# Fetching each expert pair's token rows by indirect DMA, and splitting every gate chunk, in a one-core hybrid attention, mLSTM and mixture-of-experts layer

## The chip, the cores and the metric

The kernel runs on one core of one Trainium2 chip, in one launch. The metric is the device time of that launch in microseconds; the kernel before has a median of 1496.52 us over three runs (1495.86 to 1496.99). All stage times below are counted in us from the start of the profiled span.

## The reference, cut to what matters

256 tokens of width 2048 go through one layer in float32: a big input projection, sparse attention, an mLSTM, a gated mix and an output projection, a layer norm (h), and then the part that the change touches:

```python
def hier_moe(x, w_grp, b_grp, w_exp, b_exp, w_gate, w_up, w_down):
    grp_prob = softmax(x @ w_grp + b_grp)              # 4 groups, the best one is taken
    g_p, g_idx = top_k(grp_prob, 1)
    e_p, e_idx = top_k(softmax(in_grp), 2)             # 2 of the 4 experts of that group
    e_p = e_p / sum(e_p)
    h = silu(x @ w_gate[e]) * (x @ w_up[e]) * combine[e]   # e = 0..15, FF = 512
    return h @ w_down[e], summed over the experts

ff = hier_moe(h, ...)
ple = (p @ w_ple) * sigmoid(h @ w_ple_gate)            # w_ple_gate is 2048 x 2048
h = layer_norm(DN_ALPHA * h + ff + ple, ln2_g, ln2_b)
```

Each token takes 2 of 16 experts, so 512 token slots are in use out of 16 x 64 that the kernel keeps. On the inputs used, the experts receive 13, 21, 18, 18, 34, 39, 35, 48, 30, 34, 32, 24, 40, 51, 38 and 37 tokens.

## The kernel before, in words

**Projections.** Until about 916 us the weights of the projections pass through a ring in SBUF; ScalarE copies each tile to a rounded high part (float32r), VectorE subtracts it for the low part, and TensorE makes three float32r matmuls (high x high, low x high, high x low) in place of one float32 matmul. The change leaves that part alone.

**Between the projections and the experts** (916 to 947 us) the rows are normalized (`RES`, which SyncE also writes to the output tensor in DRAM as a parking place, line 452), turned on TensorE (`row_turn`, line 875) and kept as `hT`; the router is computed; VectorE makes `selg`, a 0/1 matrix of tokens against the 64 slots of each of a group's 4 experts (`select`, line 2247). The rows are also split into `h1h` (ScalarE, `high`, line 1502) and `h1l` (VectorE, `h1_low`, line 2155).

**The experts** are taken in 8 pairs, two pairs to a group. `up(n)` has 8 slots: each slot loads 1 MiB of one weight of each of the two experts (2 MiB) and multiplies it with `xg`, the turned rows of the pair's slots; `down(n)` has 4 slots of 2 MiB. The written order is up 0, up 1, down 0, up 2, down 1, up 3, ... down 5, up 7, down 6, down 7. `xg` is made by selection products: for a group, `gather_pair` (line 976) multiplies `h1h` and `h1l` with `selg`, 8 pairs of feature tiles of 8 float32r matmuls with 256 columns, and ScalarE and VectorE add gain and bias while they copy the result out (`gained`, lines 1563 and 2262). Group 0 is gathered before and inside up 0 (`first_pairs`), group g at the start of down(2g-2), between its slots. `scatter` (lines 1107, 1108) adds a pair's outputs to the token rows with the turned matrix `selT`.

**The gate product** h @ w_ple_gate is cut into 16 chunks: one loaded early (`EW`), 15 that travel in the ring at fixed slots (`CHUNKS_IN`). Chunks 0 to 8 are float32 matmuls with `hT` (`ple_rows`, line 928), which the trace records as two instructions each; chunks 9 to 14 are split like the projections (`gate_high` line 1592, `gate_low` line 2339, `split_rows` lines 950 to 952), after `turned_high` and `turned_low` have split `hT` itself in down 4.

**The ring.** `moe_ring` has 8 places of 1 MiB and 207 loads pass through it, in the order in which TensorE uses them. SyncE issues load m once TensorE has used load m-8:

```python
            def ring_load(m, dst, src):
                ...
                else:
                    sp.wait_ge(ring_used, m - RING + 1)
                sp.dma_start(dst, src).then_inc(ring_in[m % RING], 16)
```

So the first 8 loads are in before the experts start, and the other 199 follow TensorE's progress. No planner decides anything: each engine's order is the order of the code.

**The end** (1456 to 1498 us): the last four down slots with scatters between them (`down_last`, line 1092), `last_scatter`, the statistics, the second norm and the output.

Of the kernel before, what the change touches and what calls it, by code (L numbers as in the profile page):

```python
# [68 lines left out]
SPLIT_FROM = 9  # L69
# [68 lines left out]
def build(nc, x, p, w_in, kv_norm, w_ukv, m_i_bias, m_f_bias, w_proj_a, w_proj_m, w_out, ln1_g, ln1_b,  # L138
          w_grp, b_grp, w_exp, b_exp, w_gate, w_up, w_down, w_ple, w_ple_gate, ln2_g, ln2_b, out):
    with ExitStack() as ctx:  # L140
# [46 lines left out]
        GH = at("gate_hi", [2, D], Z1 + 16384, F32R)  # L187
# [34 lines left out]
        xg = at("xg", [KT, EPG * CAP], Z3)  # L222
# [43 lines left out]
        lgc, lbc, fold = tiny(KT), tiny(KT), tiny(32)  # L266
        flag = at("flag", [2], ZS + 3072, I32)

# [10 lines left out]
        ident_ready, const_ready, identr_ready = sem("ident_ready"), sem("const_ready"), sem("identr_ready")  # L279
# [27 lines left out]
        h1_hi, h1_lo, res_gain, res_ready = sem("h1_hi"), sem("h1_lo"), sem("res_gain"), sem("res_ready")  # L307
# [190 lines left out]
        def _(pl):  # L498
# [50 lines left out]
            def deviation(n):  # L549
# [6 lines left out]
            deviation(1)  # L556
            g.iota(iota[:], pattern=[[1, CAP]], base=0, channel_multiplier=0,
                   allow_small_or_imprecise_dtypes=True).then_inc(iota_ready, 1)
# [6 lines left out]
        def _(pe):  # L565
# [366 lines left out]
            def ple_chunk(at, b):  # L932

                i = CHUNK_OF[at]
                pe.wait_ge(ple_ev, i + 1)
                if i < SPLIT_FROM:
                    ple_rows(landed_load(("ple", i, 0, 0)), b, (i + EARLY) % 4, True, True).then_inc(ring_used, 1)
                else:
                    split_rows(i, b).then_inc(ring_used, 1)

            def split_rows(i, b):

                j, s = i - SPLIT_FROM, LOAD_AT["ple", i, 0, 0] % RING
                pe.wait_ge(split_hi, j + 2)
                pe.wait_ge(split_lo, j + 2)
                for t in range(4):
                    k, c = 4 * ((i + EARLY) % 4) + t, slice(t * NC, t * NC + NC)
                    for a in range(NT):
                        r = slice(a * P, a * P + P)
                        mm(B[b + a][:, :], hTh[:, k, r], GH[:, j % 2, c], start=t == 0, stop=False)  # L950
                        mm(B[b + a][:, :], hTl[:, k, r], GH[:, j % 2, c], start=False, stop=False)
                        last = mm(B[b + a][:, :], hTh[:, k, r], RL0[:, s, c], start=False, stop=t == 3)
# [10 lines left out]
            def weight_table(bank, s):  # L963

                for pair in range(2):
                    for a in range(NT):
                        last = mm(B[bank][:, 4 * pair:4 * pair + 4], selg[:, a, pair * P:pair * P + P].bitcast(F32),
                                  combw[:, 4 * a:4 * a + 4], start=a == 0, stop=a == 1)
                last.then_inc(s, 1)

# [15 lines left out]
            def gather(g, pairs):  # L986

                for i in pairs:
                    if i < 2:
                        pe.wait_ge(selT_c, 2 * g + i + 1)  # L990
                    elif i % 2:
                        pe.wait_ge(g_dve, 4 * (g - 1) + i // 2)
                    else:
                        pe.wait_ge(g_act, 8 + 4 * (g - 1) + i // 2)
                    gather_pair(i, B[i % 2]).then_inc(g_mm, 1)

            def first_pairs(q):
# [9 lines left out]
            def up_slot(w, i, b0, e0):  # L1007

                for t in range(4):
                    k = 4 * (i // 2) + t  # L1010
                    for e in range(2):
                        last = mm(B[b0 + i % 2][CAP * e:CAP * e + CAP, :], xg[:, k, (e0 + e) * CAP:(e0 + e) * CAP + CAP],  # L1012
# [3 lines left out]
            def up(n):  # L1016

                b, other = 2 * (n % 2), 2 * ((n + 1) % 2)
                if n and n % 2 == 0:
                    pe.wait_ge(g_act, 8 + 4 * (n // 2))  # L1020
                    pe.wait_ge(g_dve, 4 * (n // 2))
                if n:
                    pe.wait_ge(ple_ev, max(chunks_in("up", n - 1) + chunks_in("down", n - 2), default=-1) + 2)
                for i in range(UP_SLOTS):
                    w = landed_pair("up", n, i)
                    if n == 0 and i % 2 == 0:
                        pe.wait_ge(g_act, i + 2)
                    up_slot(w, i, b, 2 * (n % 2)).then_inc(ring_used, 2)
                    if n == 0 and i in (1, 3):
                        if i == 1:  # L1030
                            pe.wait_ge(combined, 1)
                            weight_table(5, selT_mm)
                        first_pairs(i // 2 + 2)
                    if n == 0 and i == 6:
                        ple_rows(EW[:, 0, :], 2, 0, True, True, (1, 2, 3)).then_inc(early_used, 1)
                    if i == 2:
                        if n:
# [30 lines left out]
            def down(n):  # L1068

                pe.wait_ge(e_Tc, n + 1)  # L1070
                if n:
                    pe.wait_ge(y_add, 2 * CHUNKS * n)
                for k in range(DOWN_SLOTS):
# [4 lines left out]
                    if n % 2 == 0 and n < NP - 2:  # L1078
                        if k == 0:
                            pe.wait_ge(ple_ev, max(chunks_in("up", n + 1)) + 2)  # L1080
                            group_rows(n // 2 + 1)
# [86 lines left out]
            with pe.Else():  # L1168
                pe.wait_ge(split_lo, len(CHUNKS_IN) - SPLIT_FROM + 2)
                pe.wait_ge(y_add, 2 * CHUNKS * NP)  # L1170
                for r in range(3):
                    with pe.Fori(0, GROUPS) as g:
# [10 lines left out]
                        for pair in range(2):  # L1183
# [8 lines left out]
                            for i in range(UP_SLOTS):  # L1192
                                up_slot(landed_over(i), i, 0, 2 * pair).then_inc(ring_used, 2)
# [18 lines left out]
        def _(ac):  # L1212
# [286 lines left out]
            def high(a):  # L1499

                ac.wait_ge(z_ready, NT)
                fn(h1h[:, a, :, :].rearrange("p t q -> p q t"), RES[:, a, :].rearrange("p (q t) -> p q t", t=KT),
                   ACT.Copy).then_inc(h1_hi, 1)
# [10 lines left out]
            high(0)  # L1514
            pp_copy(4)
            pp_copy(5)
            high(1)
            pp_copy(6)
            pp_copy(7)
# [25 lines left out]
            def weight_table(ready, r0, bank, s, weights):  # L1545

                ac.wait_ge(ready, r0 + 2)
                for e in range(2):
                    last = fn(weights[CAP * e:CAP * e + CAP, :], B[bank][CAP * e:CAP * e + CAP, e:e + 12:6], ACT.Copy)
                last.then_inc(s, 1)  # L1550

            def group_tables(g):
# [4 lines left out]
                row_table(selT_mm, 2 * g, 0, selT_c, g % 2)  # L1557
                weight_table(selT_mm, 2 * g, 1, selT_c, cg[:, 2 * (g % 2):2 * (g % 2) + 2])

            def gained(i, b):  # L1560

                for k in (2 * i, 2 * i + 1):
                    last = fn(xg[:, k, :], b[:, k % 2 * TOK:k % 2 * TOK + TOK], ACT.Identity, bias=lbc[:, k:k + 1],
# [3 lines left out]
            def gathered(g):  # L1567

                used("up", 2 * g - 1, UP_SLOTS - 1)
                for i in range(0, 8, 2):  # L1570
                    ac.wait_ge(g_mm, 8 * g + i + 1)
                    gained(i, B[0]).then_inc(g_act, 1)

# [937 lines left out]
```

## Time and profile before

| | before |
|---|---|
| median of 3 runs | 1496.52 us |
| the profiled execution, its own time | 1499.46 us |
| its span, first to last instruction | 1497.7 us |
| TensorE busy | 1464.7 us (98%) |
| VectorE, ScalarE, GpSimd busy | 706.8, 513.2, 57.1 us |
| bytes moved by DMA | 405.92 MB, mean 271 GB/s |
| mean granted TensorE clock | 0.998 |

TensorE's busy time is an average over a projection part, in which the DMA engines are about half busy, and the expert part, in which the page's DMA digits stand at 9 throughout. A matmul's printed duration is longer than the time from one to the next, because they are pipelined: pitches are read from start times.

### The profile page before, as it was taken

To read this page: it belongs to the slowest core of one execution; us is meant where nothing else is said; L and a number is where in the kernel's file an instruction comes from. 1 tells how busy PE (TensorE), PEld (TensorE's weight loads), DVE (VectorE), ACT (ScalarE), POOL (GpSimd) and SP (SyncE) were. 2 spreads that over 40 slices of the span, in tenths; PEclk is the share of its full clock that TensorE was granted. 3 is DMA by queue.
4 is the path that set the end of the run, shared out by engine and by line. 5 is a ranking of instruction groups with operands and counts; after the bars stand their busy time and mean duration, and the time that the engine had idled before them with its cause. 6 is when DMAs were issued, how large, how long until landed. Compare 5 with 4: busy or idle time off the path is not lost.

```text
span 1497.7 us, 16743 instructions
## 1 busy us (share of the span) xinstructions
PE 1464.7 (98%) x6572; PEld 997.8 (67%) x6572; DVE 706.8 (47%) x974; ACT 513.2 (34%) x690; POOL 57.1 (4%) x63
## 2 busy tenths in 40 slices
PE   9999999999999999999999999999989998999998
PEld 7887788888788888888888886534424533444443
DVE  5546676467656665454555655421221221143336
ACT  4444444455554454434445343401000201031111
POOL 0000000043300000000000000000000000000000
PEclk9999999999999999999999999999999999999999
DMA  9654586754454675565566957599999999999994
GB/s 310 200 172 165 168 238 198 218 194 157 145 171 141 202 237 190 187 197 195 196 204 231 368 202 257 241 414 421 407 399 411 389 390 418 410 389 418 416 401 173
DMA packets 138287, 405.92 MB, mean 271 GB/s; under 512 B 14296, under 2 KB 18016, under 8 KB 113248
## 3 DMA queue, kind: packets, MB, share of 16 engines
q1 hardware_dynamic: 129472, 396.52, 72.6%
q10 hardware_dynamic: 8736, 8.33, 1.7%
q8 instruction: 51, 0.84, 0.2%
q14 instruction: 28, 0.23, 0.1%
HBM read 392.76 MB, written 4.20 MB: 265 GB/s over the span
## 4 chain that ended last, share of the span: by engine, by line
PE 90%; DMA 7%; DVE 1%; ACT 1%; issue 1%; SPq 0%; POOL 0%; DVEq 0%; POOLq 0%; ACTq 0%
PE bank L574 19%; PE bank L575 19%; PE bank L579 19%; PE bank L1012 11%; PE bank L1064 5%; PE bank L928 4%; DMA moe_ring<-in_w_gate_dram 4%; DMA moe_ring<-in_w_ple_gate_dram 2%; PE bank L976 2%; PE bank L1092 1%; PE bank L1107 1%; PE bank L1108 1%; DMA moe_ring<-in_w_down_dram 1%; PE bank L733 1%; PE bank L950 1%; PE bank L755 1%
## 5 line engine op out<-in xcount | busy, mean ns | idle before, releaser
L1715 DVE TENSOR_TENSOR w_lo<-w_ring,w_hi 128x1024 fp32r<-128x1024 f32 (+1 forms) x312 | 381.5, 1225 | 286.0 <-ACT w_hi L1228 284.9
L1228 ACT ACTIVATE w_hi<-w_ring 128x1024 fp32r<-128x1024 f32 (+1 forms) x312 | 327.3, 1051 | 328.9 <-PE bank L579 328.9
L574 PE MATMUL bank<-w_hi,xT_hi 128*128 128x512 f32 (+1 forms) x864 | 344.3, 399 | 1.8 <-ACT w_hi L1228 1.8
L575 PE MATMUL bank<-w_hi,xT_lo 128*128 128x512 f32 (+1 forms) x864 | 334.6, 387 | 0.0
L1012 PE MATMUL bank<-moe_ring,xg 128*64 128x512 f32 x1024 | 226.4, 595 | 9.8 <-DMA moe_ring<-in_w_gate_dram 7.1
L579 PE MATMUL bank<-w_lo,xT_hi 128*128 128x512 f32 (+1 forms) x864 | 229.2, 387 | 0.0
L574 PEld LDWEIGHTS bank<-w_hi,xT_hi 128*128 128x128 f32 x864 | 162.3, 188 | 38.6 <-issue 4.6
L575 PEld LDWEIGHTS bank<-w_hi,xT_lo 128*128 128x128 f32 x864 | 162.4, 188 | 32.8 <-issue 1.9
L579 PEld LDWEIGHTS bank<-w_lo,xT_hi 128*128 128x128 f32 x864 | 161.5, 188 | 33.2 <-DVE w_lo L1715 0.4
L1012 PEld LDWEIGHTS bank<-moe_ring,xg 128*64 128x64 f32 x1024 | 72.9, 137 | 156.3 <-issue 155.9
L1064 PE MATMUL bank<-moe_ring,moe_hiddenT 128*64 128x512 f32 x448 | 100.5, 595 | 3.8 <-DMA moe_ring<-in_w_down_dram 3.7
L2318 DVE TENSOR_TENSOR res<-res,bank 128x512 f32<-128x512 f32 x62 | 38.5, 681 | 104.4 <-issue 80.3
L1064 PEld LDWEIGHTS bank<-moe_ring,moe_hiddenT 128*64 128x64 f32 x448 | 31.7, 137 | 63.7 <-issue 62.4
L928 PE MATMUL bank<-moe_ring,h1T 128*128 128x512 f32 x144 | 63.4, 593 | 0.0
L2281 DVE TENSOR_TENSOR ple_sig<-bank,ple_sig 128x512 f32<-128x512 f32 x24 | 15.5, 686 | 81.3 <-PE bank L928 58.3
L574 PE MATMUL bank<-w_hi,mixT_hi 128*128 128x512 f32 x128 | 50.1, 391 | 0.0
L575 PE MATMUL bank<-w_hi,mixT_lo 128*128 128x512 f32 x128 | 49.8, 389 | 0.0
L574 PE MATMUL bank<-w_hi,yaT_hi 128*128 128x512 f32 x128 | 49.8, 389 | 0.0
L575 PE MATMUL bank<-w_hi,yaT_lo 128*128 128x512 f32 x128 | 49.8, 389 | 0.0
L574 PE MATMUL bank<-w_hi,ymT_hi 128*128 128x512 f32 x128 | 49.8, 389 | 0.0
L575 PE MATMUL bank<-w_hi,ymT_lo 128*128 128x512 f32 x128 | 49.8, 389 | 0.0
L928 PEld LDWEIGHTS bank<-moe_ring,h1T 128*128 128x128 f32 x144 | 27.2, 190 | 31.6 <-issue 31.0
(292 smaller groups left out, 1360.9 us busy)
## 6 DMA issues: line engine op xcount, KB each, us to landing
w_ring<-in_w_in_dram SPq DMA_DIRECT2D x103, 1024.0 KB, 5.0
moe_ring<-in_w_gate_dram SPq DMA_DIRECT2D x64, 1024.0 KB, 9.8
moe_ring<-in_w_up_dram SPq DMA_DIRECT2D x64, 1024.0 KB, 10.6
moe_ring<-in_w_down_dram SPq DMA_DIRECT2D x64, 1024.0 KB, 10.5
w_ring<-in_w_proj_a_dram SPq DMA_DIRECT2D x16, 1024.0 KB, 5.0
w_ring<-in_w_proj_m_dram SPq DMA_DIRECT2D x16, 1024.0 KB, 5.0
w_ring<-in_w_out_dram SPq DMA_DIRECT2D x16, 1024.0 KB, 5.3
moe_ring<-in_w_ple_gate_dram SPq DMA_DIRECT2D x15, 1024.0 KB, 13.1
```

What stands on the lines that cost most here:

```text
L574: mm(b, lh(k, m), WH[:, s, kk, 0:width], start=start and kk == 0, stop=False)
L575: mm(b, ll(k, m), WH[:, s, kk, 0:width], start=False, stop=False)
L579: last = mm(b, lh(k, m), WL[:, s, kk, 0:width], start=False, stop=stop and kk == 1)
L733: last = mm(B[4 + j][:, r * w:r * w + w], aqT[:, 4 * (u % 4) + 2 * j + r, a * P:a * P + P], kT[:, 0:w], start=True, stop=True)
L928: ins = mm(B[b + a][:, :], hT[:, k, a * P:a * P + P], w[:, t * NC:t * NC + NC], start=first and t == 0, stop=last and t == 3)
L976: last = mm(b[:, kk * TOK:kk * TOK + TOK], src[:, a, 2 * i + kk, :], selg[:, a, :], start=part == 0 and a == 0, stop=part == 1 and a == 1)
L1012: last = mm(B[b0 + i % 2][CAP * e:CAP * e + CAP, :], xg[:, k, (e0 + e) * CAP:(e0 + e) * CAP + CAP], w[e][:, t * NC:t * NC + NC], start=k = ...
L1064: last = mm(B[4 + c][CAP * e:CAP * e + CAP, :], src[:, k, CAP * e:CAP * e + CAP], w[e][:, c * NC:c * NC + NC], start=k == 0, stop=k == 3)
L1228: fn(WH[:, h % 4, :, 0:width], W32[:, h // 2, 2 * (h % 2):2 * (h % 2) + 2, 0:width], ACT.Copy).then_inc(hi_ready, 1)
L1715: v.tensor_tensor(WL[:, h % 4, :, 0:width], W32[:, h // 2, 2 * (h % 2):2 * (h % 2) + 2, 0:width], WH[:, h % 4, :, 0:width].bitcast(F32), A ...
L2281: last = v.tensor_tensor(psg[:, a, :], B[b + a][:, :], psg[:, a, :], ALU.add)
L2318: v.tensor_tensor(r, r, B[b0 + a][:, :], ALU.add).then_inc(y_add, 1)
```

## The change

The selection products go. Instead, a list of token numbers per slot is made, and GpSimd fetches each pair's 128 slot rows (8 KiB each) from the output tensor in DRAM by an indirect DMA, which leaves out the slots whose list entry is 4096 or more. For groups 1 to 3 an empty slot gets 4096; for group 0 the list is a plain product, so an empty slot gets 0 and row 0 is fetched for it: 128 rows for each of pairs 0 and 1. TensorE turns the fetched rows, 16 transposes of 128x128 to a pair, and ScalarE and VectorE copy them into `xg` with gain and bias. All 15 ring chunks of the gate product are split in three passes; `hT` is split before up 0 and `gate_hi` has one buffer for two.

```diff
-SPLIT_FROM = 9
+FAR = 4096
...
-        GH = at("gate_hi", [2, D], Z1 + 16384, F32R)
+        ZG = at("z_slots", [D], Z1 + 16384)
+        GH = at("gate_hi", [D], Z1 + 24576, F32R)
...
+            for n in range(NP):
+                pl.wait_ge(listed, n // 2 + 1)
+                if n == 0:
+                    pl.wait_ge(z_moved, 16)
+                    pl.wait_ge(pp_mm, 8)
+                elif n == 1:
+                    pl.wait_ge(split_hi, 1)
+                    pl.wait_ge(split_lo, 1)
+                    pl.wait_ge(early_used, 1)
+                    pl.wait_ge(rows_in, 16)
+                else:
+                    pl.wait_ge(g_mm, 4 * n)
+                g.indirect_dma_start((ZG if n else ZG0)[:], None, out[0], bass.IndirectOffsetOnAxis(ap=idx[:, n:n + 1], axis=0),
+                                     bounds_check=TOK - 1, oob_is_err=False).then_inc(rows_in, 16)
...
-                if i < SPLIT_FROM:
-                    ple_rows(landed_load(("ple", i, 0, 0)), b, (i + EARLY) % 4, True, True).then_inc(ring_used, 1)
-                else:
-                    split_rows(i, b).then_inc(ring_used, 1)
+                split_rows(i, b).then_inc(ring_used, 1)
...
+            def pair_turn(n, q, b0):
 
                 if q == 0:
-                    pe.wait_ge(pp_c, 8)
-                pe.wait_ge(h1_lo, q + 1)
-                for i in (2 * q, 2 * q + 1):
-                    if i >= 2:
-                        pe.wait_ge(g_act, i - 1)
-                    gather_pair(i, B[6 + i % 2]).then_inc(g_mm, 1)
+                    pe.wait_ge(rows_in, 16 * (n + 1))
+                if q >= 2:
+                    pair_evacuated(n, q - 2)
+                elif n == 1:
+                    pair_evacuated(0, q + 2)
+                z = (ZG if n else ZG0).rearrange("p (q t) -> p t q", t=KT)
+                for kk in range(4):
+                    last = nc.tensor.transpose(B[b0 + q % 2][:, kk * P:kk * P + P], z[:, 4 * q + kk, :], ident[:])
+                last.then_inc(g_mm, 1)
...
             def down(n):
...
-                        if k < 3:
-                            gather(n // 2 + 1, ((0, 1), (2, 3, 4), (5, 6, 7))[k])
...
+                    if k >= 2 and n < NP - 2:
+                        pe.wait_ge(e_hid, n + 2)
+                        for q in (2 * k - 4, 2 * k - 3):
+                            pair_turn(n + 2, q, 2 * ((n + 1) % 2))
...
             pe.wait_ge(sel_ready, 1)
+            first_list()
             row_table(4, selT_mm)
-            pe.wait_ge(h1_hi, NT)
-            first_pairs(0)
-            first_pairs(1)
+            ple_rows(EW[:, 0, :], 2, 0, True, True, (1, 2, 3)).then_inc(early_used, 1)
+            pe.wait_ge(pp_c, 8)
+            for q in range(4):
+                pair_turn(0, q, 6)
...
             select(0)
-            for q in range(4):
-                h1_low(q)
+            slot_list(0)
             combine()
             overflow()
+            turned_low()
+            gained(0, 1, 7)
+            gained(0, 3, 7)
             residual(0)
             residual(1)
+            gained(1, 1, 7)
+            gained(1, 3, 7)
```

Where the instructions stand. TensorE between the router and up 0, before: the selection products (L976) stand ahead of the first weights (L1012).

```order
L928 MATMUL bank<-ple_early,h1T 128x512
L960 MATMUL bank<-ident_r,moe_sel 128x128 [waits sel_ready]
L960 MATMUL bank<-ident_r,moe_sel 128x128 x3
L976 MATMUL bank<-moe_sel,h_hi 128x256 [waits h1_lo,pp_copied,h1_hi]
L976 MATMUL bank<-moe_sel,h_hi 128x256
L976 MATMUL bank<-moe_sel,h_lo 128x256 x2
...
L1012 MATMUL bank<-moe_ring,xg 64x512 [waits gathered_act,ring_in1,ring_in0]
L1012 MATMUL bank<-moe_ring,xg 64x512 x7
```

The same place after the change (L1001 is the slot list, L952 the rest of the early chunk, L1034 a turn of fetched rows, L1042 the first weights):

```order
L1001 MATMUL bank<-small,moe_sel 128x1 [waits sel_ready]
L1001 MATMUL bank<-small,moe_sel 128x1 x3
L986 MATMUL bank<-ident_r,moe_sel 128x128 x4
L952 MATMUL bank<-ple_early,h1T 128x512 x6
L1034 MATMUL bank<-ident,z_slots_first 128x128 [waits slot_rows_in,pp_copied]
L1034 MATMUL bank<-ident,z_slots_first 128x128 x7
L1034 MATMUL bank<-ident,z_slots_first 128x128 [waits gathered_act]
L1034 MATMUL bank<-ident,z_slots_first 128x128 x3
L1034 MATMUL bank<-ident,z_slots_first 128x128 [waits gathered_dve]
L1034 MATMUL bank<-ident,z_slots_first 128x128 x3
L1042 MATMUL bank<-moe_ring,xg 64x512 [waits gathered_act,ring_in1,ring_in0]
```

The rest of the early chunk moved from slot 6 of up 0 to a place ahead of it, and the first weights now stand behind the landing of pair 0's rows and behind two evacuations.

TensorE in down 0, after the change: the tables of group 1 stand ahead of the first slot, and the turns of pair 2 behind slots 2 and 3 (L1092 is a down slot).

```order
L986 MATMUL bank<-ident_r,moe_sel 128x128 [waits sel_ready,ple_evac,e_T_copied]
L986 MATMUL bank<-ident_r,moe_sel 128x128 x3
L993 MATMUL bank<-small,moe_sel 128x5 x4
L1092 MATMUL bank<-moe_ring,moe_hiddenT 64x512 [waits ring_in2,ring_in1]
...
L1092 MATMUL bank<-moe_ring,moe_hiddenT 64x512 [waits ring_in6,ring_in5]
L1092 MATMUL bank<-moe_ring,moe_hiddenT 64x512 x7
L1034 MATMUL bank<-ident,z_slots 128x128 [waits slot_rows_in,e_hid]
L1034 MATMUL bank<-ident,z_slots 128x128 x7
L1092 MATMUL bank<-moe_ring,moe_hiddenT 64x512 [waits ring_in0,ring_in7]
L1092 MATMUL bank<-moe_ring,moe_hiddenT 64x512 x7
```

Before, 64 selection matmuls stood between the slots at this place, and the tables behind slot 0.

## Rows read from the trace of the kernel before

**Rows 1.** The page, part 2: share of the span in 40 slices.

```profile
PE   9999999999999999999999999999989998999998
DMA  9654586754454675565566957599999999999994
```

**Rows 2.** The stages: busy time of each engine, granted clock, DMA share, GB/s.

```profile
core 0: us, PE busy (x) PEld busy (x) DVE busy (x) ACT busy (x) POOL busy (x), PEclk, DMA share, GB/s
940.00:951.00 11.00, 10.29 (x60) 6.34 (x60) 9.67 (x20) 6.32 (x13) 0.00 (x0) 1.00 0.01 2
952.00:1466.00 514.00, 494.04 (x2190) 217.52 (x2187) 130.24 (x198) 73.69 (x120) 0.00 (x0) 1.00 1.00 406
1096.00:1126.00 30.00, 24.74 (x114) 8.97 (x111) 3.03 (x8) 2.67 (x5) 0.00 (x0) 1.00 1.02 418
1240.00:1265.00 25.00, 19.90 (x88) 7.97 (x85) 4.96 (x8) 2.66 (x5) 0.00 (x0) 1.00 1.02 418
1366.00:1420.00 54.00, 50.19 (x226) 23.63 (x223) 14.31 (x18) 9.65 (x13) 0.00 (x0) 1.00 1.02 418
1085.00:1096.00 11.00, 11.00 (x48) 3.81 (x48) 5.97 (x12) 1.65 (x2) 0.00 (x0) 1.00 0.94 358
```

**Rows 3.** DMA from 952 to 1466 us: packets and bytes.

```profile
DMA packets 37454, 208.92 MB, mean 406 GB/s; under 512 B 3178, under 2 KB 3178, under 8 KB 14900
```

**Rows 4.** TensorE's waits from 951 to 1473 us: total, times, longest.

```profile
PE bank L1012 <- DMA moe_ring<-in_w_gate_dram: 7.1, 6, 1.3
PE bank L950 <- DVE gate_lo L2339: 5.5, 4, 2.5
PE bank L1064 <- DMA moe_ring<-in_w_down_dram: 3.7, 3, 1.3
PE bank L1012 <- DMA moe_ring<-in_w_up_dram: 2.6, 2, 1.3
```

**Rows 5.** Timeline of TensorE: start us, us, engine, line, what, count [idle before].

```profile
923.33 3.98 PE L875 MATMUL bank<-ident,res 128*128 128x128 f32 x32 [0.29 <-DVE res L2144]
...
940.80 0.96 PE L960 MATMUL bank<-ident_r,moe_sel 128*128 128x128 f32 x4
...
946.70 7.09 PE L1012 MATMUL bank<-moe_ring,xg 128*64 128x512 f32 x32
953.71 1.06 PE L967 MATMUL bank<-small,moe_sel 128*128 128x4 f32 x8
...
976.28 5.42 PE L928 MATMUL bank<-ple_early,h1T 128*128 128x512 f32 x12
...
1034.51 0.40 PE L976 MATMUL bank<-moe_sel,h_lo 128*128 128x256 f32 x2
1034.74 0.40 PE L976 MATMUL bank<-moe_sel,h_hi 128*128 128x256 f32 x2
...
1126.99 7.03 PE L928 MATMUL bank<-moe_ring,h1T 128*128 128x512 f32 x16
...
1351.88 0.39 PE L950 MATMUL bank<-gate_hi,h1T_hi 128*128 128x512 f32 x1
...
1357.41 7.09 PE L1012 MATMUL bank<-moe_ring,xg 128*64 128x512 f32 x32
...
1472.74 3.65 PE L1092 MATMUL bank<-moe_ring,moe_hiddenT 128*64 128x512 f32 x16
```

**Rows 6.** SyncE's DMA issues in order of time.

```profile
923.30 0.40 SPq L452 DMA_DIRECT2D out_dram<-res  x1
950.39 0.81 SPq L445 DMA_DIRECT2D moe_ring<-in_w_gate_dram  x2
```

**Rows 7.** The page, part 6: DMA issues, KB each, median us from issue to landing.

```profile
moe_ring<-in_w_down_dram SPq DMA_DIRECT2D x64, 1024.0 KB, 10.5
w_ring<-in_w_proj_a_dram SPq DMA_DIRECT2D x16, 1024.0 KB, 5.0
```

**Rows 8.** VectorE's timeline from the router to 950 us.

```profile
938.75 1.39 DVE L2247 TENSOR_SCALAR moe_sel<-iota,small 128x64 fp32r<-128x64 f32 x8
940.06 7.96 DVE L2155 TENSOR_TENSOR h_lo<-res,h_hi 128x512 fp32r<-128x512 f32 x8
947.92 0.17 DVE L2219 TENSOR_REDUCE small<-small 128x2 f32<-128x8 f32 x1
```

**Rows 9.** Groups of ScalarE and VectorE instructions: busy us, mean ns of one.

```profile
L1667 ACT ACTIVATE rstd_diagonal<-ident,small 128x128 f32<-128x128 f32 x2 | 0.8, 402 | 7.3 <-POOL small L561 7.3
L2331 DVE TENSOR_TENSOR h1T_lo<-h1T,h1T_hi 128x1024 fp32r<-128x1024 f32 x4 | 4.6, 1220 | 2.9 <-ACT h1T_hi L1579 2.9
L1592 ACT ACTIVATE gate_hi<-moe_ring 128x1024 fp32r<-128x1024 f32 x12 | 12.0, 1048 | 54.9 <-DMA moe_ring<-in_w_ple_gate_dram 54.9
```

More of the change, by code:

```diff
@@ L949, in split_rows @@
                         r = slice(a * P, a * P + P)
-                        mm(B[b + a][:, :], hTh[:, k, r], GH[:, j % 2, c], start=t == 0, stop=False)
-                        mm(B[b + a][:, :], hTl[:, k, r], GH[:, j % 2, c], start=False, stop=False)
+                        mm(B[b + a][:, :], hTh[:, k, r], GH[:, c], start=t == 0, stop=False)
+                        mm(B[b + a][:, :], hTl[:, k, r], GH[:, c], start=False, stop=False)
+                pe.wait_ge(split_lo, i + 2)
+                for t in range(4):
+                    k, c = 4 * ((i + EARLY) % 4) + t, slice(t * NC, t * NC + NC)
+                    for a in range(NT):
+                        r = slice(a * P, a * P + P)
                         last = mm(B[b + a][:, :], hTh[:, k, r], RL0[:, s, c], start=False, stop=t == 3)
@@ L966, in weight_table, with first_list @@
                     for a in range(NT):
-                        last = mm(B[bank][:, 4 * pair:4 * pair + 4], selg[:, a, pair * P:pair * P + P].bitcast(F32),
-                                  combw[:, 4 * a:4 * a + 4], start=a == 0, stop=a == 1)
+                        last = mm(B[bank][:, 5 * pair:5 * pair + 5], selg[:, a, pair * P:pair * P + P].bitcast(F32),
+                                  wtk[:, 5 * a:5 * a + 5], start=a == 0, stop=a == 1)
                 last.then_inc(s, 1)
+            def first_list():
+                for pair in range(2):
+                    for a in range(NT):
+                        last = mm(B[5][:, 480 + pair:481 + pair], selg[:, a, pair * P:pair * P + P].bitcast(F32), tok[:, a:a + 1],
+                                  start=a == 0, stop=a == 1)
+                last.then_inc(list_mm, 1)
             def gather_pair(i, b):
@@ L1513, in _ @@
                 last.then_inc(hT_act, 1)
[L1514 to L1519, printed above, removed]
+            for q in range(4):
+                pp_copy(4 + q)
+                last = turned_high(q)
+            last.then_inc(split_hi, 1)
             def used(kind, n, i):
@@ L1548, in weight_table @@
                 for e in range(2):
-                    last = fn(weights[CAP * e:CAP * e + CAP, :], B[bank][CAP * e:CAP * e + CAP, e:e + 12:6], ACT.Copy)
+                    last = fn(weights[CAP * e:CAP * e + CAP, :], B[bank][CAP * e:CAP * e + CAP, e:e + 14:7], ACT.Copy)
                 last.then_inc(s, 1)
@@ L1557, in group_tables, with gained @@
                 row_table(selT_mm, 2 * g, 0, selT_c, g % 2)
+                ac.wait_ge(listed, g + 1)
                 weight_table(selT_mm, 2 * g, 1, selT_c, cg[:, 2 * (g % 2):2 * (g % 2) + 2])
-            def gained(i, b):
+            def gained(n, q, b):
+                ac.wait_ge(g_mm, 4 * n + q + 1)
+                for kk in range(4):
+                    k = 4 * q + kk
+                    last = fn(xg[:, n % 2, k, :], B[b][:, kk * P:kk * P + P], ACT.Identity, bias=lbc[:, k:k + 1],
+                              scale=lgc[:, k:k + 1])
+                last.then_inc(g_act, 1)
@@ L1562, in gained, with gained_over @@
+            def gained_over(i, b):
                 for k in (2 * i, 2 * i + 1):
-                    last = fn(xg[:, k, :], b[:, k % 2 * TOK:k % 2 * TOK + TOK], ACT.Identity, bias=lbc[:, k:k + 1],
+                    last = fn(xgo[:, k, :], b[:, k % 2 * TOK:k % 2 * TOK + TOK], ACT.Identity, bias=lbc[:, k:k + 1],
                               scale=lgc[:, k:k + 1])
                 return last
[L1567 to L1572, printed above, removed]
@@ L2361, in _ @@
             for kind, n in ORDER[:-1]:
+                if kind == "down" and n % 2 == 0 and n < NP - 2:
+                    slot_list(n // 2 + 1)
                 for slot in range(SLOTS_OF[kind]):
@@ L2372, in _ @@
                         ple_part((i + EARLY) // 4)
-                    if kind == "up" and n >= 6 and slot == 2:
-                        gate_low(10 if n == 6 else 13)
                 if kind == "up":
                     hidden(n)
-                    if n >= 6:
-                        gate_low(11 if n == 6 else 14)
                     if n % 2 == 0 and n < NP - 2:
```

178 lines of the change are left out of this document (81 added, 97 removed).

## The prediction

> **What bounds the kernel now.** I began with the page's slices: TensorE shows 9 nearly everywhere, but from slice 27 on the DMA digits are 9 as well [rows 1]. So the expert part is short of two things at once, and the view that tells them apart is the stages. Where TensorE waits for weights (1096 to 1126, 1240 to 1265, 1366 to 1420 us), the DMA engines move 418 GB/s at a share of 1.02, and no stage shows more: that is their ceiling here. Over the whole of 952 to 1466 us they move 406 GB/s at 1.00, TensorE being busy for 494 of the 514 us; where TensorE holds the ring places (1085 to 1096) it is 358 at 0.94 [rows 2]. The waits agree: TensorE waits 13.4 us in all for weights, never over 1.3 us at once, and 5.5 us for VectorE's low part of a gate chunk [rows 4]. The bytes of the stage, 208.92 MB [rows 3], are just the 199 loads of 1 MiB (208.7 MB) that follow TensorE, so the last of them lands at about 1466 us, and TensorE begins the last down slot only at 1472.74 [rows 5]. The two engines are thus near a tie: a stream that could end earlier by its rate, and TensorE a little behind it at the end.
>
> **What TensorE saves.** A selection matmul follows the last by 0.12 us (1034.51 to 1034.74 for two, [rows 5]); 256 of them are 30.7 us. In their place come 8 x 16 transposes at 3.98/32 = 0.124 us [rows 5], 15.9 us. A float32 chunk is 16 records in 6.96 us (7.03 of which the last end overlaps), a split one 1351.88 to 1357.41 less a restart, 5.45 us [rows 5]: 9 chunks give 13.6 us. The slot list adds 1 us, being as large as the weight table of 1.06 us [rows 5]. Together TensorE has 27 us less to do.
>
> **What that is worth is read from the stream,** not from that sum. Four terms.
>
> *The start, +5.0 us.* The first ring issue of the stage comes at 950.39 [rows 6], when slot 0 of up 0, begun at 946.70 [rows 5], is used. After the change slot 0 waits for this: `selg` ready at 940.1 [rows 8]; the list product 1 us, to 941.8; its copy, to 942.1; the fetch of 1 MiB. No row shows an indirect DMA. A load takes 5.0 us from issue to landing in the projections and 10.5 in a full queue [rows 7], and the engines stand idle here (2 GB/s, [rows 2]), so it lands between 944.6 (its bytes alone at 418 GB/s) and 952.6; I take 947.1, the nearest row. TensorE fills that time with 5.42 us of the early chunk [rows 5], to 947.6, which is work moved and no loss. Then two turns, to 948.6. What is late next is VectorE: after the list copy come the combine and overflow steps (2 us), the low part of `hT`, 4 x 1.22 = 4.9 us [rows 9], to 950, then four evacuations of 128x128, under 0.4 each by ScalarE's 128x128 copy of 402 ns [rows 9], to 951.3, then the last turn: up 0 begins at 951.7, not 946.7. The selection products inside up 0 and the early chunk there are gone, but the stream doesn't gain from it: it starts with the first used slot. Pair 1's fetch is issued at about 950 and lands before the ring asks for much, so it costs nothing; without that gap it would be 2.5 us.
>
> *The stream's idle time, -15.0 us.* 208.7 MB take 499 us at 418 GB/s, against 514 now. With 27 us less work TensorE releases places fast enough nearly everywhere.
>
> *The rows, +11.0 us.* GpSimd fetches pairs 2 to 7 while the stream runs. The 16 experts' counts put 442 token rows of 8 KiB into them, 3.62 MB: 8.7 us at 418 GB/s. That is the lower end. The upper is that each of the six costs as much as a whole load of 1 MiB, 6 x 2.5 = 15.0 us: taken slots are always the first of each expert's 64, so the same partitions get the rows each time, and a load of 128 partitions has landed only when its slowest share has. I take 11, between them.
> The Trainium skill has a price for that: its page "DMA: Bandwidth & Descriptors", section "The descriptor swizzle", gives each DMA engine eight fixed partitions, by which the busiest one (partitions 64 to 67 and 96 to 99) gets 42 of the 442 rows where the mean is 27.6. By that skill page the term would be an estimated 13 us and the sum 2 us longer; no row here shows an engine by itself.
>
> *The end, -5.0 us.* TensorE is now 6.6 us behind the last landing. With the saved work it should be 1 to 2 us behind: the last four down slots and three scatters between them take it as long as 8 loads take, and chunk 14 ahead of them still has its wait, up to 2.5 us [rows 4], since ScalarE makes that chunk's high part (2 x 1.05 us, [rows 9]) only after the hidden turn.
>
> *A rest, +1.0 us,* for chunks behind which the ring still stands full. Of the other edits, the turns of pair n+2 behind slots 2 and 3 of down n wait for fetched rows and ScalarE's evacuations; an even pair's fetch is issued at the start of that down, some 10 us (three slots of 3.5 us) ahead, against 5.0 to 10.5 us for landing [rows 7], and a short wait there is covered by the stream, which has eight places in hand. If that cover is gone each of three such waits costs what it lasts. ScalarE's and VectorE's nine more chunk splits (2.1 and 2.4 us each, [rows 9]) fall beside TensorE's slots; both are under 26% busy there [rows 2]. GpSimd has nothing else in its queue until the last norm.
>
> Sum: 5.0 - 15.0 + 11.0 - 5.0 + 1.0 = **-3.0 us**. The profiled execution took 1499.46 us, so the same sum gives 1496.5 there; that execution lies 2.9 us above the median of 1496.52, from which the forecast is **1493.5 us**. A measurement of this kernel can tell about 0.2% (3 us) from no change, so this forecast lies on that bound.
>
> **Rivals.**
> 1. *The gather is late (slower).* From the landing, up 0 needs two turns (1.0), an evacuation by each of ScalarE and VectorE (1.6) and two more turns (1.0), 3.6 us; so from a landing at 948 us on, 6 us after the list, the rows and not VectorE set the start, and every us of theirs moves the whole stream by one. GpSimd has never issued such a DMA in this trace, and it has to make 128 row addresses. At 10 us from list to landing (952.1) up 0 begins at 955.7, 4 us more, 1497.5; at 13 us it is 7 more, 1500.5. For it: an operation without a row. Against: idle DMA engines. Chance of over 9 us, 0.22, with some 1500.5.
> The Trainium skill's page "SBUF — State Buffer", section "SBUF: two separate sides", warns that GpSimd can't write descriptors while VectorE holds the port that the two share. VectorE's instructions beside the first fetch are tiny ones until 945 us, then four of 1.22 us [rows 9] until 950. As a mechanism of this kernel: a fetch whose addresses are written only behind these lands at about 952.5 (950 and the 2.5 us of its bytes), and up 0 begins 4.4 us later than I have it, 1498. No row here shows GpSimd held up by VectorE, and I give that 0.05 of the 0.22.
> 2. *The rows cost as whole loads,* by the partitions or because empty slots aren't left out after all: the rows' term is 15 or more, 1497.5, no change. For it: the same slots are full each time. Against: eight loads in flight even things out. 0.20.
> 3. *TensorE's saving comes through whole:* 27 us less 5, 1474. The waits for weights of 13.4 us [rows 4] and the 1.02 share speak against it. 0.03.
> 4. *The stream fills up better than I think,* rows at their 8.7 us and the start only 3 us later: -8 us, 1488.5. 0.13.
>
> The forecast's own case has 0.42 and its range is 1490.5 to 1496.5. The range for 8 in 10 reaches to half of rival 4 and into rival 1: 1487 to 1502. Faster by over 0.2%: half of the forecast's case and a bit (0.25), rivals 3 and 4 (0.16), 0.41. Within 0.2%: the rest of the forecast's case (0.17), most of rival 2 (0.16) and a little of rival 1 (0.02), 0.35. Slower: 0.24.
>
> **What would show it.** After the change TensorE should be clearly less busy from 952 us on, with some 35 to 50 us of waits for weights in pieces under 2 us, and the DMA engines at 415 to 420 GB/s over the whole stage. Up 0 should begin at 951 to 953 us, the wait ahead of it ending with VectorE's evacuation or with the rows. The bytes of the stage should be near 212.5 MB; near 215 would say that empty slots are fetched. The last down slot should begin within 2 us of the last landing. The prediction is wrong if GB/s stays at 406, if up 0 begins after 956, or if TensorE waits for fetched rows by more than 3 us in a down.

## The result, and the profile after

The changed kernel is slower: 1505.3 us (median of 4 runs, 1504.21 to 1507.19) against 1496.19 us (4 runs, 1491.39 to 1496.99), a ratio of 1.0075 with a 95% interval of 1.0063 to 1.0088. The forecast was 1493.5 us with a range up to 1502; the time lies above it. The profiled execution took 1505.65 us, its span is 1503.9 us (before: 1497.7).

The page of the changed kernel, parts 1 to 3:

```profile
PE 1451.9 (97%) x6524; PEld 1000.3 (67%) x6524; DVE 730.1 (49%) x1028; ACT 526.9 (35%) x730; POOL 65.6 (4%) x73
...
DMA  8654586754444776565566956699999999999994
...
DMA packets 139440, 411.65 MB, mean 274 GB/s; under 512 B 14750, under 2 KB 18470, under 8 KB 113702
...
q0 software_dynamic: 1152, 5.72, 1.0%
```

Queue q0 is new: 5.72 MB are 698 rows of 8 KiB, the 256 of group 0 and the 442 of the others. Empty slots are left out, as the change says.

The stages of the changed kernel (same columns as in [rows 2]):

```profile
940.00:953.60 13.60, 10.58 (x44) 6.24 (x42) 8.20 (x22) 5.54 (x12) 2.27 (x2) 0.96 0.32 99
953.60:958.50 4.90, 4.90 (x19) 1.61 (x20) 1.79 (x5) 4.45 (x5) 0.00 (x0) 0.76 0.38 154
960.00:1472.00 512.00, 475.63 (x2138) 218.11 (x2135) 151.82 (x247) 87.89 (x156) 5.95 (x6) 0.98 1.02 415
```

The stream is full now: 415 GB/s at 1.02 where [rows 2] had 406 at 1.00, and TensorE is busy for 476 of 512 us instead of 494 of 514. That part of the forecast is there, though TensorE was to save 27 us and not 18; part of what is missing is its granted clock, 0.98 over this stage and 1.00 before (see the last section). The start is not as forecast. TensorE around up 0 (start us, us, engine, line, what, count, idle before):

```profile
942.57 5.37 PE L952 MATMUL bank<-ple_early,h1T 128*128 128x512 f32 x12
949.81 1.14 PE L1034 MATMUL bank<-ident,z_slots_first 128*128 128x128 f32 x8 [1.87 <-DMA z_slots_first<-out_dram,slot_rows]
952.09 1.67 PE L1034 MATMUL bank<-ident,z_slots_first 128*128 128x128 f32 x8 [1.15 <-ACT xg L1595]
953.69 8.20 PE L1042 MATMUL bank<-moe_ring,xg 128*64 128x512 f32 x32
...
1478.66 3.65 PE L1121 MATMUL bank<-moe_ring,moe_hiddenT 128*64 128x512 f32 x16
```

and the engines ahead of it, VectorE's list, GpSimd's fetch and SyncE's first issue of the stage:

```profile
942.27 0.16 DVE L2272 CAST slot_rows<-bank 128x2 int32<-128x2 f32 x1 [2.04 <-PE bank L1001]
...
943.38 1.28 POOL L580 DMA_INDIRECT z_slots_first<-out_dram,slot_rows  x1 [22.36 <-DVE slot_rows L2272]
...
958.50 0.81 SPq L451 DMA_DIRECT2D moe_ring<-in_w_gate_dram  x2
```

The rows are there at 949.8 us, 7.4 us after the list, of which 1 us passes before GpSimd begins. Up 0 begins at 953.69, not at 946.70, and its first two slots take 8.1 us instead of 7.0: the granted clock is 0.76 in that stretch, partly at 1.2 GHz and partly at 2.4. The first ring issue comes 8.1 us later than in [rows 6]. The last down slot begins 5.9 us later than in [rows 5].

Where TensorE waits in the changed kernel, from 940 us on:

```profile
PE bank L1042 <- issue: 12.8, 7, 3.3
PE bank L971 <- ACT gate_hi L1616: 8.8, 8, 2.7
PE bank L1042 <- DMA moe_ring<-in_w_up_dram: 8.6, 8, 2.4
PE bank L1092 <- DMA moe_ring<-in_w_down_dram: 4.8, 4, 2.6
```

"Issue" means that the profile names no releaser; these waits stand at up slots, as those for weights do, and I count them as such. The wait for `gate_hi` is one for ScalarE's high part of a gate chunk.

### The profile page after: what moved, and what is told of

Read it like the earlier page. It is cut to its first block, busy times and chain, and to the rows that moved or that the text cites. A ratio compares the mean times of both kernels' runs of the same rounds, so it can differ in the third digit from the quotient of the medians.

```text
span 1503.9 us, 16809 instructions
## 1 busy us (share of the span) xinstructions
PE 1451.9 (97%) x6524; PEld 1000.3 (67%) x6524; DVE 730.1 (49%) x1028; ACT 526.9 (35%) x730; POOL 65.6 (4%) x73
## 3 DMA queue, kind: packets, MB, share of 16 engines
q0 software_dynamic: 1152, 5.72, 1.0%
## 4 chain that ended last, share of the span: by engine, by line
PE 88%; DMA 8%; issue 1%; ACT 1%; DVE 1%; SPq 0%; POOL 0%; POOLq 0%; ACTq 0%; DVEq 0%
PE bank L598 19%; PE bank L599 19%; PE bank L603 19%; PE bank L1042 13%; DMA moe_ring<-in_w_up_dram 6%; PE bank L1092 4%; PE bank L971 2%; PE bank L978 2%; PE bank L972 2%; ACT gate_hi L1616 1%; PE bank L1121 1%; DMA moe_ring<-in_w_ple_gate_dram 1%; DMA moe_ring<-in_w_down_dram 1%; PE bank L757 1%; PE bank L1136 1%
## 5 line engine op out<-in xcount | busy, mean ns | idle before, releaser
L1042 PE MATMUL bank<-moe_ring,xg 128*64 128x512 f32 x1024 | 237.6, 615 | 22.5 <-issue 12.8
L1042 PEld LDWEIGHTS bank<-moe_ring,xg 128*64 128x64 f32 x1024 | 76.5, 141 | 166.9 <-issue 166.1
L1092 PE MATMUL bank<-moe_ring,moe_hiddenT 128*64 128x512 f32 x448 | 101.4, 603 | 4.8 <-DMA moe_ring<-in_w_down_dram 4.8
L1092 PEld LDWEIGHTS bank<-moe_ring,moe_hiddenT 128*64 128x64 f32 x448 | 32.3, 138 | 65.1 <-issue 64.5
L2279 DVE TENSOR_SCALAR xg<-bank,small 128x128 f32<-128x128 f32 x64 | 21.9, 403 | 109.5 <-PE bank L1034 109.5
L1595 ACT ACTIVATE xg<-bank,small 128x128 f32<-128x128 f32 x64 | 24.1, 458 | 113.4 <-PE bank L1034 113.4
L971 PE MATMUL bank<-gate_hi,h1T_hi 128*128 128x512 f32 x120 | 48.5, 404 | 8.8 <-ACT gate_hi L1616 8.8
L1616 ACT ACTIVATE gate_hi<-moe_ring 128x1024 fp32r<-128x1024 f32 x30 | 30.0, 1048 | 76.6 <-DMA moe_ring<-in_w_ple_gate_dram 63.7
L2356 DVE TENSOR_TENSOR gate_lo<-moe_ring,gate_hi 128x1024 fp32r<-128x1024 f32 x30 | 35.3, 1218 | 35.6 <-ACT gate_hi L1616 35.6
```

The costliest lines, as they stand in the source:

```text
L971: mm(B[b + a][:, :], hTh[:, k, r], GH[:, c], start=t == 0, stop=False)
L1042: last = mm(B[b0 + i % 2][CAP * e:CAP * e + CAP, :], rows[:, k, CAP * e:CAP * e + CAP], w[e][:, t * NC:t * NC + NC], start=k == 0, stop=k ...
L1092: last = mm(B[4 + c][CAP * e:CAP * e + CAP, :], src[:, k, CAP * e:CAP * e + CAP], w[e][:, c * NC:c * NC + NC], start=k == 0, stop=k == 3)
L1616: last = fn(GH[:, c], RW[:, m % RING, c], ACT.Copy)
L2356: last = v.tensor_tensor(RL0[:, s, c], RW[:, s, c], GH[:, c].bitcast(F32), ALU.subtract)
```

## A second profile of the kernel before

The profiles differ by 6.2 us, the medians by 9.1. So I took the kernel before once more.

> The kernel before once more, for a second profile. The span of the first one is 1497.7 us where the runs of this kernel have a median of 1494 to 1496.5. If the first profile was a long execution, this one's span is 1490 to 1496 us, and the place of the difference shows what the extra us of the changed kernel's median over its profiled difference are; if the span is 1497 to 1498 again, the profiler itself adds them.

Its span is 1494.4 us. TensorE's last down slot and the second ring issue of the stage (in the first profile at 1472.74 and 953.82):

```profile
952.97 0.81 SPq L445 DMA_DIRECT2D moe_ring<-in_w_up_dram  x2
...
1469.24 3.65 PE L1092 MATMUL bank<-moe_ring,moe_hiddenT 128*64 128x512 f32 x16
```

The first profile was a long execution: 0.9 us came before the stream, 2.6 us of the rest within it. Against the second one the changed kernel's last down slot is 9.4 us later and its span 9.5 us longer, close to the difference of the medians. Below I use both.

## The experiments

Each ratio below is to runs of the kernel before that were taken beside that experiment; their medians lie between 1494.0 and 1495.3 us. Differences to the changed kernel are to its 1505.3 us, so they carry 1 to 2 us of doubt.

Three theories went in. **A:** the weight stream, from its first issue on, sets the pace as far as up 7, and TensorE's own work sets the rest (79 us from the last wait for weights to the last down slot); start, rows and end each count in full. **C:** a later start or added bytes are caught up on the way. **E:** it is TensorE's sum that counts.

**The rows of groups 1 to 3, taken away.**

```diff
-                    v.tensor_scalar(idx[:, 2 * g:2 * g + 2], B[1][:, 4:14:5], float(FAR), None, ALU.add).then_inc(listed, 1)
+                    v.tensor_scalar(idx[:, 2 * g:2 * g + 2], B[1][:, 4:14:5], 3.0 * FAR, None, ALU.add).then_inc(listed, 1)
```

> The changed kernel, except that the slot lists of groups 1 to 3 are out of range, so that pairs 2 to 7 fetch no row (3.62 MB less) and compute on stale rows. Theory A (the weight stream sets the pace up to up 7, and TensorE's own work of some 79 us sets the rest): the rows cost what their bytes take at 418 GB/s, 8.7 us, so 1497 us, with up 7 beginning 8 to 9 us sooner. Theory B (a fetch costs as much as a whole load of 1 MiB): 15 us less, 1490. Theory C (the rows ride in idle DMA time): under 3 us less, over 1502.

1495.72 us, 9.6 us less than the changed kernel. The stream begins at the same time and the last down slot 10.2 us sooner:

```profile
958.69 0.81 SPq L451 DMA_DIRECT2D moe_ring<-in_w_gate_dram  x2
...
1468.44 3.65 PE L1121 MATMUL bank<-moe_ring,moe_hiddenT 128*64 128x512 f32 x16
```

A holds, C falls for bytes. 3.62 MB cost 9.6 to 10.2 us, between their 8.7 us at 418 GB/s and 15. The six fetches are still made here, they only carry no row (from 960 to 1478 us):

```profile
q0 software_dynamic: 864, 0.00, 0.1%
z_slots<-out_dram,slot_rows POOLq DMA_INDIRECT x6, 7.4
```

So what this run takes away is the price of the rows' bytes, not that of a fetch as such. The kernel has every saving of the change and no row behind the start, and still is only level with the kernel before (1.0012, 1.0002 to 1.0022): the late start alone eats what TensorE saves.

**Empty slots fetched too.** The list column of `wtk` starts at 0 instead of -4096 and nothing is added, so empty slots name row 0.

> The changed kernel with empty slots of groups 1 to 3 listed as row 0, so that all 8 fetches move 128 rows: 326 rows or 2.67 MB more behind the start of up 0. Same output. Theory A (bytes at the stream's rate, 10 us for the 3.62 MB that are fetched now): 6.4 to 7.4 us slower than the changed kernel, 1511 to 1513. Theory B (each fetch costs as a whole load already, by its fullest partitions): under 2 us slower, 1507.

1508.7 us (1506.27 to 1510.76), 3.4 us more; in the profiles the last down slot is 5.2 us later, although the stream began 0.8 us sooner. The page says that the bytes moved:

```profile
q0 software_dynamic: 1152, 8.39, 1.4%
```

2.67 MB more cost 3.4 us by the medians and 6.0 us by the profiles (5.2 and the 0.8 us of the start). A had 6.4 to 7.4, B under 2, and the runs lie between them; the spread of four runs to a side (1506.27 to 1510.76 here) is as large as what would tell them apart. From no row to all rows the two steps together cost 13.0 us by the medians and 16.4 us by the profiles, and the 6.29 MB of both are 15.0 us at 418 GB/s. That a fetch costs anything beyond its bytes, or that the fullest partitions count, is not shown; nor is whether row 0, read 326 times, costs what other rows do.

**The wait for pair 0's rows, taken away.** `pair_turn(0, ...)` reads `RES[:, 0, :]` and leaves out `wait_ge(rows_in, ...)`; the fetch is still made.

> The changed kernel, except that pair 0's turns read rows that are in SBUF already (tokens 0 to 127) and don't wait for the fetch, which is still made; pair 0 computes on the wrong rows. Theory A: the first pair's fetch holds the start of the stream; up 0 begins at about 951.6 us instead of 953.7, held by VectorE's evacuation now, and the whole stream moves by the same 2 us; with the slow clock of the first slot gone, up to 1 us more: 1502 to 1503.5. Theory C (a later start is caught up, since the ring is full and TensorE was waiting for weights anyway): 1505, no change. If the start moves by x and the end by less than half of x, the start was not the cause.

1501.36 us, 3.9 less.

```profile
951.92 7.09 PE L1042 MATMUL bank<-moe_ring,xg 128*64 128x512 f32 x32
...
1474.66 3.65 PE L1121 MATMUL bank<-moe_ring,moe_hiddenT 128*64 128x512 f32 x16
```

Up 0 begins at 951.9, as forecast for a fetch that is in time (951.7), at full clock: its first two slots take 7.0 us. The first issue is 2.9 us sooner (955.61) and the last down slot 4.0. So 2.9 us of the 8.1 are the landing and the slow clock behind it, and the other 5 are the new chain itself. Most of the earlier start is in the landing of the last ring load too, 2.5 us sooner (1471.67 for 1474.21); the rest of the 4.0 is TensorE standing 3.0 us behind that landing in place of 4.5, for which I have no cause.

**ScalarE's order at the chunks.**

```diff
                     if n == NP - 2:
+                        gate_high(chunks_in(kind, n)[0])
                         hidden_turned(n + 1)
```

and likewise for the chunk behind slot 2 of each up.

> The changed kernel with ScalarE's order changed: the high part of a chunk behind slot 2 of an up, and of chunk 14 in down 6, is made ahead of the copy of the turned hidden rows, not behind it. Same output. Theory A (TensorE is the bound from slot 2 of up 7 on): its waits for the high part there, 0.82 us at chunk 12 and 2.67 us at chunk 14, go, so the end comes 3 us sooner, about 1502; the waits of this kind ahead of up 7 are worth nothing, the stream covers them. Theory D (the last landing sets the end): no change, 1505. Theory E (TensorE's sum of waits counts everywhere): all 8.8 us, 1496.5.

1502.36 us, 2.9 less. The wait for high parts goes from 8.8 to 2.4 us and the end gains 3 of the 6.4, those in the end part. The profile shows what is late next, the last loads:

```profile
PE bank L971 <- ACT gate_hi L1616: 2.4, 3, 1.2
...
PE bank L1121 <- DMA moe_ring<-in_w_down_dram: 0.6, 1, 0.6
```

**The fetched rows without the split chunks.** `ple_chunk` calls `ple_rows` for all 15; `h1T` isn't split, and `z_slots` lies where its high part was.

> The changed kernel with all 15 ring chunks as float32 products of h1T (6.96 us each on TensorE instead of 5.45 and no high or low parts), the fetched rows kept. Same output. Theory A: twelve of the 15 chunks lie where the stream sets the pace and cost next to nothing; the last three add 4.5 us to TensorE's end part and take its waits of 3.5 us for high parts away, so 1505 to 1508. Theory E (TensorE's sum counts): 15 x 1.5 = 22.6 us less the 8.8 us of waits, 1519.

1508.13 us, 2.8 more than the changed kernel. The split of the chunks, some 14 us of TensorE's work and 22 if it is counted over all 15, is worth 2.8 us at most: the profile's first ring issue is itself 1.0 us later (959.53), with a longer stretch of slow clock in slot 0. E falls, since it asked for 1519.

**Two of the last three chunks, done ahead of up 7.**

```diff
-CHUNKS_IN = (("up", 1, 4), ("up", 2, 2), ("up", 2, 5), ("up", 3, 2), ("up", 3, 5), ("up", 4, 2), ("up", 4, 5),
+CHUNKS_IN = (("up", 1, 4), ("up", 2, 2), ("up", 2, 5), ("down", 1, 1), ("up", 3, 2), ("up", 3, 5), ("up", 4, 2),
...
-             ("up", 5, 2), ("up", 5, 5), ("up", 6, 2), ("up", 6, 5), ("down", 5, 1), ("up", 7, 2), ("up", 7, 5),
-             ("down", 6, 1))
+             ("up", 4, 5), ("down", 3, 1), ("up", 5, 2), ("up", 5, 5), ("up", 6, 2), ("up", 6, 5), ("down", 5, 1),
+             ("up", 7, 2))
```

> The changed kernel with two of the last three gate chunks' places moved ahead: places (up 7, slot 5) and (down 6, slot 1) are given up for (down 1, slot 1) and (down 3, slot 1). Same output. Theory A (from up 7 on TensorE is the bound, ahead of it the stream is): TensorE gives up two chunks and the 2.7 us wait of chunk 14 in the end part and does them where it waits for weights; it can gain no more than its lag behind the last landing, 6.5 us, less 1: 5 us faster than the changed kernel, 1500, with the last down slot beginning within 1.5 us of the last landing. Theory E (it is TensorE's whole sum that counts): no change, 1505.

1503.29 us (1502.4 to 1505.37), 2 us less where I had 5. TensorE now does wait for the last loads:

```profile
PE bank L1092 <- DMA moe_ring<-in_w_down_dram: 3.4, 3, 1.4
PE bank L1121 <- DMA moe_ring<-in_w_down_dram: 1.7, 1, 1.7
```

so the place of the bound is as A says. But the last ring load landed 1.5 us later than in the changed kernel (1475.73 for 1474.21), of which 0.7 us is a later first issue (959.18), and part of the gain was given back. There was also less to gain than I thought: in the changed kernel the last down slot begins 4.5 us after that landing and not 6.5, and here 0.8.

**Group 0 by selection products again,** pairs 2 to 7 fetched; `h1T` is split behind up 0's products:

```diff
-            for n in range(NP):
+            for n in range(2, NP):
...
-            first_list()
             row_table(4, selT_mm)
-            ple_rows(EW[:, 0, :], 2, 0, True, True, (1, 2, 3)).then_inc(early_used, 1)
-            pe.wait_ge(pp_c, 8)
-            for q in range(4):
-                pair_turn(0, q, 6)
+            pe.wait_ge(h1_hi, NT)
+            first_pairs(0)
+            first_pairs(1)
```

> The changed kernel with group 0's rows made by selection products as before (no fetch for pairs 0 and 1), h1T split behind up 0's products, all else as changed. Same output. Theory A: the first issue of the ring goes back from 958.5 to 950.4 us and the whole stream with it, 8 us faster than the changed kernel, 1497.5, less up to 1 us for TensorE's 7 us of products. Theory C (a later start is caught up): under 3 us faster.

1498.79 us, 6.5 less than the changed kernel and 1.0033 (1.0023 to 1.0044) of the one before. The stream is back where it was and the end 4.8 us sooner:

```profile
953.62 0.81 SPq L452 DMA_DIRECT2D moe_ring<-in_w_up_dram  x2
...
1473.89 3.65 PE L1122 MATMUL bank<-moe_ring,moe_hiddenT 128*64 128x512 f32 x16
```

From the first issue to the last down slot it takes 523.7 us (from 950.2), the changed kernel 520.2: the earlier start is not passed on in full, 4.8 of 8.3 us in the profile and 6.5 by the medians (the profiled execution, 1500.78 us, is 2 us longer than this kernel's median). That TensorE's products in up 0 make the difference is likely, but wasn't tried.

**All three together.**

> Group 0 by products, the two chunk places moved ahead, and ScalarE's high parts behind slot 2 ahead of the turned hidden rows, all together. Same output. Theory A adds the two gains, 8 and 5 us, as they lie in different parts: 1492, some 3 us faster than the kernel before. Theory C and E: 1500 or more.

1494.98 us, 10.3 less than the changed kernel and level with the one before (1.0007, 0.9998 to 1.0017). I had 1492, from gains of 8 and 5 us that came out at 6.5 and 2 to 3. What was gained adds nearly in full, but it only makes good the cost.

**The same move of chunks in the kernel before.** Chunks 0 to 10 stay float32.

> The kernel before with the same two chunk places moved ahead (chunks 0 to 10 float32, 11 to 14 split, as their places ask). Same output. Theory A: there TensorE holds the ring in many stretches ahead of up 7 too, so 11 to 14 us of added work there push the stream back by most of that, and the gain at the end is used up: between 1493 and 1499. Theory F (the gain is in the tail alone and has nothing to do with the fetched rows): 5 us faster than the kernel before, 1490.

1492.59 us, 0.9987 of the kernel before (0.9976 to 0.9998), 1.4 us less than its median of 1493.99: the fastest kernel of this study, by little. I had it at 1493 to 1499, so here my theory was too gloomy: the stream of the kernel before took the added work without ending later. Its last load landed at 1465.18, as in the second profile of the kernel before (1465.20), though the stream began 1.2 us later (950.78). TensorE waits for the last loads at the end here too:

```profile
PE bank L1064 <- DMA moe_ring<-in_w_down_dram: 4.2, 4, 1.3
PE bank L1092 <- DMA moe_ring<-in_w_down_dram: 1.8, 1, 1.8
```

The one edit that pays, if only just, needs no fetched rows.

## Why the prediction was wrong, by its own steps

The bound was named rightly, and TensorE's 27 us of savings were rightly not counted. Of the terms of the sum four can be read off the profiles, from the first ring issue, the landing of the last ring load (1468.66 in the first profile of the kernel before, 1465.20 in the second, 1474.21 changed, 1464.89 without rows) and the last down slot. Against the second profile:

- **The start, +5.0 forecast, +9.0 measured** (+8.1 against the first profile). This is the term that failed in size, with two parts. The landing was put at 947.1 by a row of ring loads in the projections; TensorE went on with the rows at 949.8, 7.4 us after the list and not 5.0. Then ScalarE's evacuation of 1.51 us and two more turns follow it, 3.9 us where I had 3.6. Rival 1 had this mechanism and its point ("a landing at 948 us"), with 0.22 for over 9 us; at 7.4 us the start was already set by the rows. What neither had is the clock: TensorE's wait of 1.87 us and the next of 1.15 are followed by a granted clock of 0.76 in the first two slots, 1.1 us more. VectorE's low part of `hT`, which I had as the limit, ended at 949.6, just in time.
- **The stream's idle time, -15.0 and +1.0 forecast, -9.5 measured (-12.1 against the first profile).** The kernel without rows shows it alone: from first issue to last landing it takes 506.2 us, the kernel before 515.7 us in the second profile and 518.3 in the first. The 15 us rested on one long execution, and on the highest rate of three short windows for the whole stage: 208.7 MB in 499 us, where the best kernel took 506.2 from first issue to last landing.
- **The rows, +11.0 forecast, +9.5 measured** (515.7 us with rows, 506.2 without; 9.6 by the medians). Right. By the Trainium skill's page "DMA: Bandwidth & Descriptors", section "The descriptor swizzle", the estimate was 13; the measured cost lies between the bytes and that. The page describes a plain 1 MiB transfer, and no run here shows an engine by itself.
- **The end, -5.0 forecast, +0.4 measured.** This is the step that was wrong in kind. I took TensorE's lag behind the last landing for something that saved work ahead of it shrinks. It isn't: from slot 2 of up 7 on, TensorE never waits for weights, in either kernel, and the change takes nothing away there, since chunks 12 to 14 were split before and no group is gathered behind down 4. The last such wait before, and after:

```profile
1393.18 3.65 PE L1012 MATMUL bank<-moe_ring,xg 128*64 128x512 f32 x16 [0.79 <-DMA moe_ring<-in_w_gate_dram]
...
1400.04 3.65 PE L1042 MATMUL bank<-moe_ring,xg 128*64 128x512 f32 x16 [0.45 <-issue]
```

From there to the last down slot it is 79.6 us before and 78.6 after. The lag itself was also read too large: 6.6 us came from a landing at 1466, by taking the stage's 208.92 MB for ring loads alone. The two norm rows of 1 MiB each (`ln_g_rows`, `ln_b_rows`, issued at 1457.3 and 1460.0) share that stage, the last ring load landed at 1468.66, and the lag was 4.1 us. In the changed kernel it is 4.5. It is 0.8 to 0.9 us in the four kernels that moved or unblocked work behind the last wait, and 3.0 to 4.7 us in all others.

So 9.0 - 9.5 + 9.5 + 0.4 = +9.4 us, the later last down slot. The terms meet at the same three points, so that the sum closes is no test of them. Had I kept the other terms and put the end at 0 and the start at 8, the sum would have been +5.

Of the signs named in advance, the GB/s and the bytes of q0 came as said; the start, the lag at the end and the waits did not. TensorE waits 27 us for weights (not 35 to 50), in pieces of up to 3.3 us (not under 2). And the sign set for the stage's bytes would have misled: 214.60 MB from 960 to 1478 us is "near 215", which was to say that empty slots are fetched. It is the norm rows again; q0's own 3.62 MB there say that only taken slots are.

The rival that the rows cost as whole loads is out: 15 us were not to be found. So is the rival that the first fetch waits for VectorE's four long instructions (944.96 to 949.59 us): its rows moved while they ran. From 947 to 948 us:

```profile
q0 software_dynamic: 49, 0.40, 96.8%
```

All of its 1.05 MB moved between 945 and 949.6 us. The next fetch, issued at 950.56 when those four were done, took 6.3 us from issue to landing like this one. The 7.4 us are thus 1 us from the list to GpSimd, 2 us to the first bytes, and 4 to 4.5 us until the last of them are in and seen.

## What to carry to other kernels

When a stream of weights is full, work taken off the compute engine is worth only the stream's idle time, while bytes put in its place are paid at about the stream's rate (3.62 MB, 10 us), so it didn't pay here to replace matmuls by fetches through DMA engines that are full already. Ask first what sets the stream's first issue, since a delay there went through to the end nearly in full (2.5 of 2.9 us at the last landing, 6.5 of 8.3 by the medians), and then where the last wait for the stream lies: behind it the compute engine's own work counts in full, and that is where to take work away, or from where to move it forward.

## What the runs showed of the hardware

- **An indirect DMA's price.** On GpSimd it takes 1.28 us the first time and 0.99 us each later time; the first 1 MiB was usable 7.4 us after its list, with no other queue moving rows or weights. Beside the full stream a fetch of 0.46 to 0.75 MB landed 8.8 to 10.2 us after its issue, and one that carried no row still 7.2 to 7.6 us after it, with 144 packets of its own.
- **The clock after short waits.** TensorE's granted clock fell from 2.4 to 1.2 GHz for part of a slot in the expert part of the changed kernel after single waits of 2.4 to 3.3 us, and at up 0 after one of 1.87 followed by one of 1.15, where waits of about 1.3 us, one after every slot, didn't do it in the kernel before (1.00 in the stretches of [rows 2]). One of them stands behind the fetch for pair 2, in down 0; its slot took 5.35 us instead of 3.65:

```profile
1034.61 3.65 PE L1092 MATMUL bank<-moe_ring,moe_hiddenT 128*64 128x512 f32 x16 [1.26 <-DMA moe_ring<-in_w_down_dram]
1040.90 5.35 PE L1092 MATMUL bank<-moe_ring,moe_hiddenT 128*64 128x512 f32 x16 [2.63 <-DMA moe_ring<-in_w_down_dram]
```

```profile
1040.00:1046.00 6.00, 5.10 (x16) 1.78 (x16) 0.00 (x0) 0.00 (x0) 0.00 (x0) 0.72 1.01 415
```

In a full stream the slow slot costs nothing (TensorE waits less at the next one); at the head of the stream it cost 1.1 us.

The long waits come with the rows. Without them no wait for weights is over 1.5 us and the clock stays up; from 960 to 1380 us, changed and then without rows:

```profile
960.00:1380.00 420.00, 387.57 (x1745) 175.68 (x1742) 121.22 (x201) 69.93 (x126) 5.95 (x6) 0.98 1.01 416
...
960.00:1380.00 420.00, 389.73 (x1796) 178.80 (x1794) 122.01 (x204) 72.53 (x132) 5.94 (x6) 1.00 1.02 418
```

TensorE is busy for 1451.9 us in the changed kernel and 1443.7 us without rows, with the same instructions: the slow stretches are some 8 us of its work, most of it where TensorE waits for weights anyway.
